# Input columns of two layers as three fp32r products, their parts made on ScalarE and VectorE

## The reference

```python
for layer in range(DEPTH):                       # DEPTH = 2
    h = rms_norm(x, norm1_g[layer])
    cols = lambda lo, width: h @ w_in[layer][:, lo:lo + width]
    y_sb   = stick_breaking_attention(...cols(0, 768)...)
    y_rwkv = rwkv7_time_mix(cols(768, 1024), ...)
    y_moba = moba_attention(...cols(1792, 768)...)
    y_hgrn = hgrn2_mixer(...cols(2560, 1024)...)
    for n, y_n in enumerate((y_sb, y_rwkv, y_moba, y_hgrn)):
        gate = sigmoid(cols(3584 + 1024 * n, 1024))
        merged += gate * (y_n @ w_branch[layer, n])
    x = x + merged @ w_out[layer]
    h2 = rms_norm(x, norm2_g[layer])
    x = x + (silu(h2 @ w_ffn_gate[layer]) * (h2 @ w_ffn_up[layer])) @ w_ffn_down[layer]
```

## Time and profile before

| | |
|---|---|
| Median of 3 runs | 2180.26 us (2179.89 to 2181.21) |
| The profiled execution | 2178.25 us, span of its instructions 2176.4 us |
| Granted TensorE clock, mean | 0.956 of full speed |
| PE busy | 1900.0 us (87%), 11262 records |
| PEld busy | 1436.0 us (66%) |
| DVE busy | 774.2 us (36%) |
| ACT busy | 523.0 us (24%) |
| Chain that ended last | PE 61%, DMA 20%, DVE 11%, ACT 7% |

### The profile page before, as it was taken

One profiled execution on the slowest core, in us unless ns is written; L12 is line 12 of the kernel. 1 busy time (PEld: TensorE's weight loads), 2 busy tenths in 40 slices (PEclk: granted clock), 3 DMA queues, 4 the chain that ended last, 5 costly groups with the idle time before them and its releaser, 6 DMA issues.

```text
span 2176.4 us, 26092 instructions
## 1 busy us (share of the span) xinstructions
PE 1900.0 (87%) x11262; PEld 1436.0 (66%) x11262; DVE 774.2 (36%) x1312; ACT 523.0 (24%) x780; POOL 0.2 (0%) x4
## 2 busy tenths in 40 slices
PE   6999999999998999998999999998999875555555
PEld 5898876799997898766799998546788421111101
DVE  3432332556533533234355665323444200000001
ACT  2201121244432011211344463423432210000000
POOL 0000000000000000000000000000000000000000
PEclk9999999999999999999999999999999998888888
DMA  6232342465432223353745442211126899999997
GB/s 260 87 114 81 117 155 97 160 193 190 175 121 92 97 97 116 155 194 136 241 155 174 157 130 64 97 39 39 39 78 248 351 409 409 409 409 409 409 409 301
DMA packets 170323, 414.13 MB, mean 190 GB/s; under 512 B 4832, under 2 KB 61408, under 8 KB 166752
## 3 DMA queue, kind: packets, MB, share of 16 engines
q1 hardware_dynamic: 169488, 408.69, 50.7%
q10 hardware_dynamic: 720, 3.78, 0.4%
HBM read 411.41 MB, written 1.05 MB: 190 GB/s over the span
## 4 chain that ended last, share of the span: by engine, by line
PE 61%; DMA 20%; DVE 11%; ACT 7%; issue 1%; SPq 0%; ACTq 0%; DVEq 0%
PE ps L219 45%; PE ps L767 7%; DMA ring<-in_w_e_down_dram 5%; ACT rarena L213 4%; DMA high<-in_w_e_up_dram 4%; DVE rarena L178 4%; DMA high<-in_w_e_down_dram 3%; PE ps L1157 3%; PE ps L1519 2%; DMA high<-in_w_e_gate_dram 2%; DMA ring<-in_w_e_gate_dram 2%; DVE low L178 2%; DVE high L178 2%; ACT high L213 1%; DMA ring<-in_w_e_up_dram 1%
## 5 line engine op out<-in xcount | busy, mean ns | idle before, releaser
L219 PE MATMUL ps<-high,ring 128*128 128x256 f32 (+1 forms) x2016 | 483.5, 391 | 7.8 <-DMA ring<-in_w_in_dram 5.9
L219 PE MATMUL ps<-rarena 128*128 128x256 f32 (+1 forms) x3648 | 460.0, 288 | 9.6 <-DVE rarena L178 7.4
L219 PEld LDWEIGHTS ps<-rarena 128*128 128x128 f32 x3648 | 448.3, 192 | 19.6 <-DVE rarena L178 10.4
L219 PEld LDWEIGHTS ps<-high,ring 128*128 128x128 f32 x2016 | 376.2, 192 | 81.5 <-issue 19.9
L213 ACT ACTIVATE high<-ps 128x512 f32<-128x512 f32 (+2 forms) x210 | 103.1, 491 | 719.9 <-PE ps L1519 286.8
L1519 PE MATMUL ps<-high,low 128*32 128x512 f32 x1040 | 161.0, 749 | 113.3 <-DMA high<-in_w_e_down_dram 38.6
L178 DVE TENSOR_TENSOR rarena<-ring,rarena 128x2048 fp32r<-128x2048 f32 x76 | 167.3, 2201 | 137.5 <-ACT rarena L213 135.9
L1519 PEld LDWEIGHTS ps<-high,low 128*32 128x32 f32 x1040 | 31.2, 126 | 228.5 <-issue 58.9
L213 ACT ACTIVATE rarena<-ring 128x2048 fp32r<-128x2048 f32 x76 | 139.9, 1841 | 156.6 <-DMA ring<-in_w_ffn_up_dram 92.3
L178 DVE TENSOR_TENSOR high<-high,ps 128x512 f32<-128x512 f32 x52 | 35.7, 687 | 323.9 <-PE ps L1519 266.0
L767 PE MATMUL ps<-high 128*128 128x128 f32 (+6 forms) x1024 | 128.9, 298 | 15.3 <-DVE high L178 10.7
(11 more groups left out here) (147 smaller groups left out, 1349.5 us busy)
## 6 DMA issues: line engine op xcount, KB each, us to landing
ring<-in_w_in_dram SPq DMA_DIRECT2D x34, 2048.0 KB, 7.9
high<-in_w_e_gate_dram SPq DMA_DIRECT2D x22, 2048.0 KB, 24.0
high<-in_w_e_up_dram SPq DMA_DIRECT2D x22, 2048.0 KB, 23.9
high<-in_w_e_down_dram SPq DMA_DIRECT2D x21, 2048.0 KB, 24.0
ring<-in_w_mod_dram SPq DMA_DIRECT2D x12, 2048.0 KB, 8.7
ring<-in_w_ffn_gate_dram SPq DMA_DIRECT2D x22, 1024.0 KB, 5.4
ring<-in_w_ffn_up_dram SPq DMA_DIRECT2D x22, 1024.0 KB, 8.0
ring<-in_w_e_down_dram SPq DMA_DIRECT2D x11, 2048.0 KB, 24.3
```

Source lines behind the costliest of these rows:

```text
L219: ins = self.e.matmul(out, l, r, start=first and i == 0, stop=end and i == n - 1)
```

## The change

The 52 units of a layer become fp32r. ACT makes the high part of each block of 128 columns (`block_high`, 128 x 1024), DVE the low part, in place of the loaded float32 (`block_low`). PE's unit is `group3`: 24 fp32r products, 12 in a half. `B.h` becomes `hh_` and `hl_`, made beside the first four of RWKV's eight products; the parts of blocks 0 to 2 are begun beside the others.

Ring slots 0 and 1 become four quarters of 256 columns (1 MB) each. Slot 2 holds high parts: four places up to block 27, then two, since its upper half (`HALF`) becomes the slot of `w_branch[1]` and then of the modulation's loads, now 24 of 1 MB, one at a time. `high_ahead` and `low_ahead` say at which half of unit u the parts of a later block are made. With four places the high part is made in unit b-3 and the low part in unit b-2; with two the high part of block u+1 at the first half of unit u and its low part at the second. The first four halves now stand ahead of the key norm (`FIRST_PLAN`). A modulation step stands behind every fourth half in layer 0 and every second in layer 1.

```diff
--- before.py
+++ after.py
+def high_ahead(u, half):
+    if u < TWO_PLACES - 1:
+        return [u + 3] if half else []
+    return [u + 1] if TWO_PLACES < u < BLOCKS - 1 and not half else []
+def low_ahead(u, half):
+    if u < TWO_PLACES:
+        return [] if half else [u + 2]
+    return [u + 1] if TWO_PLACES < u < BLOCKS - 1 and half else []
+def beside(steps, split, u, ahead):
+    for n, _ in enumerate(steps):
+        for b in ahead(u + n // 2, n % 2):
+            split(b)
+        yield
...
-def woven(parts, other, counts):
-    for part, n in zip(parts, counts):
-        yield from part
-        for _ in range(n):
-            next(other, None)
+def woven(parts, other, every):
+    n = 0
+    for part in parts:
+        for _ in part:
             yield
+            n += 1
+            if n % every == 0:
+                next(other, None)
+                yield
...
+        slots += [slots[2][:, SLOT // 2:SLOT]]
+        HALF = NSLOT + MORE
+        QUARTERS = [HALF + 1 + i for i in range(4)]
+        slots += [slots[i // 2][:, SLOT // 2 * (i % 2):SLOT // 2 * (i % 2) + SLOT // 2] for i in range(4)]
...
+        def block_of(l, b):
+            c0, w, o = BLOCK[b]
+            i = b % 4 if b < TWO_PLACES else b % 2
+            high_ = rblocks[:, 1024 * i:1024 * i + 1024].rearrange("p (k n) -> p k n", k=8)
+            z, low_ = (halves(s_(f"{l}w{c0}")[:, 0:8 * w], 8)[:, :, o:o + 128] for s_ in (wslot, rslot))
+            return f"{l}w{c0}", z, low_, high_
...
 (SP: the loads)
+                ring_of[0] = QUARTERS
+                for o in (768, 512, 256, 0):
+                    columns(f"{l}w{768 + o}", a["w_in"][l], 768 + o, 256)
...
+                for nm, c0, w, parts in IN1:
+                    for o in range(0, w, 256):
+                        columns(f"{l}w{c0 + o}", a["w_in"][l], c0 + o, 256)
+                for n, ch in GATES[0:3]:
+                    gate(l, n, ch)
+                held[HALF] = f"{l}blk{TWO_PLACES - 1}.used"
+                branch(l, 1, at=HALF)
                 mods = modulation(l)
+                gate(l, *GATES[3])
+                for i in range(4, 9):
+                    if i < 8:
+                        gate(l, *GATES[i])
+                    for _ in range(8 // MOD_EVERY[l]):
+                        next(mods, None)
+                ring_of[0] = range(NSLOT)
+                held[0], held[1] = held[QUARTERS[1]], held[QUARTERS[3]]
+                held[2] = f"{l}fill.used"
                 for n in (0, 2, 3):
                     branch(l, n)
...
 (PE: a unit)
+                    if kind == "c":
+                        PE.wait_ge(f"{l}lo{b_}")
+                        prs = [(hi_[:, j, :], lo[:, j, :], hh_[:, j, :], hl_[:, j, :]) for j in range(8)]
...
-                    PE.group(out, prs[0:4], end=False)
+                    PE.group3(out, prs[0:4], end=False)
                     yield
-                    PE.group(out, prs[4:8], first=False).then_inc(*PE(f"{l}{nm}{i}.ps"))
+                    PE.group3(out, prs[4:8], first=False).then_inc(*PE(f"{l}{nm}{i}.ps"))
...
 (ACT and DVE: the parts of a block)
+            def block_high(l, b):
+                ld, z, low_, high_ = block_of(l, b)
+                A.wait_ge(ld, f"{fname(l - 1, FJOBS[-1])}.used" if l else None)
+                if b > 3:
+                    A.wait_ge(f"{l}blk{b - (4 if b < TWO_PLACES + 2 else 2)}.used")
+                A.act(fr(high_), z, Copy).then_inc(*A(f"{l}hi{b}"))
...
+            def block_low(l, b):
+                ld, z, low_, high_ = block_of(l, b)
+                V.wait_ge(f"{l}hi{b}")
+                low_part(low_, z, high_, f"{l}lo{b}")
...
 (DVE: beside the first products)
+                    for h in (2 * n, 2 * n + 1) if n < 4 else ():
+                        V.stt(ys[0][:, h % 2, :], x[:, h, :], pc(("norm1_g", l), h), B.rs, mul, mul).then_inc(
+                            *V(f"{l}ht{h}"))
...
+                    for h in (2 * n, 2 * n + 1) if n < 4 else ():
+                        h_low(h)
+                    if n in (4, 5):
+                        block_low(l, n - 4)
...
-MOD_COUNTS = ((1, 1, 1, 1), (2, 2, 2, 3))
-RW_PLAN = [7, 3, 1, 4, 3, 1, 1, 1, 1, 3] + 24 * [1] + [1, 1, 1, 1, 1, 3, 3, 4]
-MX_PLAN = 10 * [2] + [1], 14 * [2] + [1]
+MOD_EVERY = (4, 2)
+BLOCKS, TWO_PLACES = 52, 28
+FIRST_PLAN = [4]
+RW_PLAN = [3, 4, 3, 4, 3, 1, 1, 1, 1, 3] + 24 * [1] + [1, 1, 1, 1, 1, 2, 2, 3]
+MX_PLAN = 13 * [2] + [1], 22 * [2] + [1]
```

More of the change, by code:

```diff
@@ L391, in build @@
         B.xg = B.mg
+        place["top"] = GATES_AT
+        hh_ = shaped(rgates[:, :].bitcast(F32), [8, 256])
         B.gates = alloc(8, 256)
@@ L443, in build @@
         free_to(mark)
-        gx = [B.gates] + [alloc(8, 256) for _ in range(2)]
+        gx = [at(23304, 8, 256)] + [alloc(8, 256) for _ in range(2)]
         H = Space()
@@ L626, in load @@
                 if at is None:
-                    i = turn["n"] % NSLOT
-                    turn["n"] += 1
+                    i = next(i for i in recent if i in ring_of[0])
+                    recent.remove(i)
+                    recent.append(i)
                 S.wait_ge(held.get(i))
@@ L772, in sums, with units @@
                 PE.group(b[:, 0:N], [(ones, sq[:, i, :]) for i in range(n)]).then_inc(*PE(f"{name}.ss"))
-            def units(l, nm, c0, w, parts):
-                wt = halves(wslot(f"{l}w{c0}")[:, 0:8 * w], 8)
-                PE.wait_ge(f"{l}w{c0}")
-                o = 0
+            def units(l, nm, parts):
+                b_ = first_block[nm]
                 for i, kind in enumerate(parts):
                     b = take("p", f"{l}{nm}{i}.ps", f"{l}{nm}{i}.out")
+                    out = b[:, 0:256]
@@ L780, in units @@
                     if kind == "c":
-                        out = b[:, 0:256]
-                        prs = [(wt[:, j, o:o + 128], B.h[:, j, :]) for j in range(8)]
-                        o += 128
+                        done = [b_]
+                        ld, z, lo, hi_ = block_of(l, b_)
+                        PE.wait_ge(f"{l}lo{b_}")
+                        prs = [(hi_[:, j, :], lo[:, j, :], hh_[:, j, :], hl_[:, j, :]) for j in range(8)]
+                        b_ += 1
                     else:
@@ L792, in units @@
+                    yield
+                    PE.group3(out, prs[4:8], first=False).then_inc(*PE(f"{l}{nm}{i}.ps"))
+                    for n in done:
+                        PE.mark(f"{l}blk{n}.used")
+                        if n % 2:
+                            PE.mark(f"{l}w{BLOCK[n][0]}.used")
                     yield
-                PE.mark(f"{l}w{c0}.used")
             def proj(l):
                 for nm, c0, w, parts in IN1:
-                    yield from units(l, nm, c0, w, parts)
+                    yield from units(l, nm, parts)
@@ L799, in gate @@
             def gate(l, n, ch):
-                yield from units(l, f"g{n}{ch}", gate_col(n, ch), 512, "cccc")
+                yield from units(l, f"g{n}{ch}", "cccc")
             def modulation(l):
@@ L1167, in tensor_program @@
                 mods = modulation(l)
-                fill = [proj(l)] + [gate(l, n, ch) for n in (1, 0) for ch in range(2)]
-                fill += [woven([gate(l, n, ch) for n in (2, 3) for ch in range(2)], mods, MOD_COUNTS[l])]
+                fill = [proj(l)] + [gate(l, n, ch) for n, ch in GATES[0:3]]
+                fill += [woven([gate(l, n, ch) for n, ch in GATES[3:]], mods, MOD_EVERY[l])]
+                mix([iter(range(1))], fill, FIRST_PLAN, False)
                 mix([rw], fill, RW_PLAN, False)
```

142 lines of the change are left out of this document (78 added, 64 removed).

## The result

The changed kernel takes 2203.89 us (median of 4 runs, 2202.49 to 2207.39), the kernel before 2180.07 in the same job. The ratio is 1.0113, 95% interval 1.0095 to 1.0130: slower by 1.1%, where 2138 and faster were forecast. The profiled execution has a span of 2203.3 us against 2176.4, at a mean granted clock of 0.941 against 0.956.

A forecast was written before the change was run, and what follows sets the result against it. PE's own work was taken as the bound. Gains of 69.1 us (56.4 + 6.8 + 5.9) less losses of 27.3 gave 41.8 us, so 2136.5 for the profiled execution and 2138 for the median; range 2114 to 2164.

The forecast's parts named there:

- The product: Layers' fill units on PE: each half 1.46 us instead of 1.73, 208 halves, 56.4 us less PE work; the main term.
- The parts: 104 weight blocks' high parts on ACT (110 us) and low parts on DVE (128 us), covered in the level loop.
- KB: Behind the key norm: the bonus product and KB's transposes wait for a late chain, 1.5 us per layer, 3 lost.
- X0: Four low parts make DVE the bound before X0; PE's wait grows from 0.69 to about 2.0 us, 2.6 lost.
- The rope: Worst mixer step, where PE's wait grows from 1.14 to 2.6 us; beside the mixers 4 us a layer, 8 lost.
- Rival (b): Fill tied to two in-order queues waits behind late mixer steps; gain 30 us less, 2168; chance 0.13.
- modulation's loads: 24 loads of 1 MB in one half slot; 16 loads wait 0.3 us each, 5 us lost.
- rival (c): Serial half slot: layer 1's modulation loads cost 5.1 us each for 16, giving 2215; chance 0.05.
- First products: RWKV's first products: 1.2 us more wait in layer 0, 2.1 in layer 1, 3.3 lost.
- The key norm: Four halves ahead of the key norm leave 1.0 of 7.8 us of waits, 6.8 gained.
- Branch 0: Its weight load is issued when PE needs it; net 2.7 us a layer, 5.4 lost.
- The clock: Lower granted clock behind branch 0's wait, 1.9 us, counted in branch 0's term.

The follow-up runs named there:

- raw_three: Changed kernel with no high or low parts of weight blocks made, its three fp32r products kept (output not the reference's): 2166.2 us, ratio 0.9962 to the kernel before.
- hybrid: Changed kernel with four places mended, and from block 32 on one f32 product, with modulation (two loads a step) and plan of before: 2155.84 us, ratio 0.9902.
- hybrid_three: `hybrid` with three fp32r products from block 32 on and no parts made for them (output not the reference's): 2138.12 us, ratio 0.9825.
- raw_one: `raw_three` with one f32 product per unit instead of three; the feed-forward products became f32 too, so its total of 2287.28 us tells nothing.
- hybrid_pieces: `hybrid` with the forget gates where the change has them and layer 0's one-time preparation cut in pieces behind KB: 2148.23 us, ratio 0.9879.
- raw_mixers: Changed kernel with parts made for blocks 0 to 27 only; from 28 on products read h's low parts as weights: 2178.34 us, ratio 1.0005.
- three_single: `hybrid_three` with modulation as one load a step and the changed kernel's plan taken back: 2164.04 us, ratio 0.9938.
- three_plan: `hybrid_three` with only the changed kernel's plan beside the mixers taken back, modulation still two loads a step: 2155.1 us, ratio 0.9901.

## Why the prediction was wrong

By spans: forecast -41.8, measured +26.9, 68.7 us apart. Of these the parts are 22.6, 38.6 measured less 16 forecast; the other 46 are lost without any part. By the stages of `raw_three`, 31 of the 46 lie beside the mixers (13.5 lost where the forecast's terms give a gain of about 17) and 9 between the decay product and branch 1 (32.0 gained of 41.4).

**The product: right.** A half is 1.43 to 1.45 in place, and one f32 product against three is worth 33.6 of 34.6 us up to branch 1 (from the runs without parts) and 16 to 18 of 21.6 beside the mixers (`hybrid` and `hybrid_three`). With the change's own plan and loads (`raw_one` and `raw_three`) only 8.4 of the 21.6 appeared there; which of the two takes the rest was not told apart.

**The parts: 38.6 us, not 16.** I had 2.4 for block 0's low part, 3 before KB, 2.6 at X0 and 8 beside the mixers. X0's wait became 2.73 in both layers, so 4.1 in all. KB waited 6.91 and 3.80 where 1.5 each were taken; without parts 4.9 of the 6.9 stay, and 1.8 of the 3.8, so the parts are 2.0 us in each layer. The preparation on DVE is another 3.1 in layer 0 (`hybrid_pieces` takes it away). What is left, 1.8 a layer, I put down to the shorter fill; no run shows it. Beside the mixers the parts cost 13 to 21. The step that failed is "Elsewhere DVE's step of 1 to 2 us plus 1.23 fits under 2.9 us of unit and about 1 to 2 of step": I asked whether the fill's product would wait for its part, and it hardly does (9.1 us in both layers). It is the mixer's own operation, queued behind a part it has no use for, that comes late. One such place, in layer 0 of the changed kernel; between the rows shown stand only weight loads, evictions and the next block's high part:

```profile
264.50 1.06 ACT L213 ACTIVATE rring<-ring 128x1024 fp32r<-128x1024 f32 x1
...
265.59 1.23 DVE L178 TENSOR_TENSOR rring<-ring,rring 128x1024 fp32r<-128x1024 f32 x1 [2.69 <-ACT rring L213]
...
266.24 1.16 PE L825 MATMUL ps<-low,high 128*128 128x128 f32 x8 [1.45 <-ACT high L213]
...
266.85 1.49 DVE L2360 COPY_PREDICATED high<-low,ps 128x512 f32<-128x512 int32 x2
...
268.44 0.89 DVE L178 TENSOR_TENSOR high<-high 128x256 f32<-128x256 f32 x2
...
269.48 1.87 PE L825 MATMUL ps<-high 64*128 64x128 f32 x14 [2.08 <-DVE high L178]
```

On ACT the high part stands ahead of the eviction for which PE waits 1.45 us. DVE stands idle 2.69 us at the head of its queue, since the low part's high part is not made yet; the mixer's masked copy and what PE needs come behind it, and PE waits 2.08. In `raw_mixers`, without the parts, the first of PE's two waits is 0.36 us and the second is gone. The rope, which I called the worst step, waited 1.34 us in layer 0 and 3.10 in layer 1, where 2.6 was the forecast. Rival (b) named that queue, at 30 us for the two layers, and it was given 0.13.

**The plan and the grain of modulation: not in the sum at all.** This error is as large as that of the parts. I priced modulation's loads (5 us; PE waited 6.7 for them, so rival (c) is out) and left out that its eight steps of 1.04 us stand where four of twice that size stood, and that more fill goes to the first steps: together 24 us, shown by `three_single`; how they share it is open. "Those 2.68 + 1.9 go, since the modulation row is now copied earlier" was the sign of it: the copy moved before something else, and costs 3.89.

**First products: 3.3 forecast.** In layer 0 I did not count the wait for parameters at the head of ACT's queue, on which DVE now depends. In layer 1 no such wait stands, and PE still waited 6.38 us where the forecast came to about 4.1. There I added DVE's durations to 3.15 us a product, and the trace has 3.61 from one to the next, longer than PE's 3.5; four times the difference is 1.8 of the missing 2.3. The kernel before showed the gaps: a product with 1.81 us of operations on DVE took 2.03 in layer 1 (642.61 to 644.64). `starts`, which mends the parameters' wait and the place of block 0's parts, gains 16 us; the two were mended together, and their shares are not told apart.

**The key norm: nearly right.** 0.43 and 1.22 us of wait are left, forecast 1.0 in all; but PE reached it later in the first place.

**Branch 0: right in size.** 5.00 and 4.84 us of DMA wait, then 40 records in 11.44 us in layer 1 at a low clock. The gain that was to stand against it was the row copy's, above.

**The clock.** I put 1.9 us a layer for it, behind one wait. Many of the added waits were followed by such a stretch. The changed kernel behind waits of 1.45 and 2.08 us at 266 and 269 (length, busy PE, granted clock, DMA, GB/s), with the stretches around it:

```profile
260.00:268.00 8.00, 5.95 (x44) 1.00 0.72 262
268.00:276.00 8.00, 6.52 (x38) 0.57 0.01 2
276.00:284.00 8.00, 7.60 (x60) 1.00 0.58 198
```

0.57 is close to the lower level, 1.2 of 2.4 GHz; 38 instructions pass where 60 pass behind it. The first part of layer 0 is the same: 0.85 over the 22.6 us behind the decay product's wait of 8.62 (43.6 to 66.2), where the kernel before has 0.99 behind its wait of 1.97 (37.6 to 54.7). But not every wait is followed by it. In the changed kernel the 8 us behind 2.73 us before X0, in both layers, and behind 3.10 us at 891.6 were granted 1.00; those behind 2.63, 3.56 and 4.49 us 0.79, and those behind 3.52 and 3.89 us 0.50 and 0.57. I can't say from the length of a wait what follows it, and the cautions above show the clock differing where the waits are alike.

The range, 2114 to 2164, took the terms' bounds, but the bounds of terms that are not in the sum can't widen it; slower had 0.06.

## What to carry to other kernels

- Work that is "hidden" on an in-order engine is paid by what is queued behind it. For each added operation ask which later operation of that queue another engine waits for, and look at the wait at the head of the queue as well: here an early wait for parameters was harmless until another engine's work was put behind it.
- If a change re-cuts a list of fill (smaller pieces, other counts a step), price the list as a part of its own, also where no operation is added. A shorter product is worth its time only while the fill still stands where the dependent chain would wait.
- Use the split first where the helpers have room: here up to branch 1 (64 halves a layer). Beside the mixers the parts cost 13 to 21 us and the product saves 16 to 18, so there it hardly pays at best; the run that would settle it was not made.

## What was not expected of the hardware

- A wait of 2 to 4 us of PE was often, not always, followed by a stretch at a lower granted clock, and the loss there can be as large as the waits. In layer 0's mixers' stage the same 980 or so instructions took 137.44 us in `three_plan` and 129.90 in `hybrid_three`. Over both layers of `three_plan` and `three_single`, 23.5 of the 41.2 us lost against `hybrid_three` are busy time and 17.7 are waits.
- With the same program and nearly the same waits in a stage, the mean clock of two executions was 0.93 and 0.96, or 0.89 and 0.95, and the stage 4 and 7 us longer; why is open.
